# Turning the first expert pair's activations and running its down product before the second pair's rows are turned, with the loads in that order

## The reference

```python
for e in range(N_EXPERTS):
    h = jax.nn.silu(xt @ lp['w_e_gate'][e]) * (xt @ lp['w_e_up'][e])
    y = y + combine[:, e:e + 1] * (h @ lp['w_e_down'][e])
```

## Time and profile before

| what | us |
|---|---|
| median of 3 runs | 783.74 |
| lowest and highest | 783.07, 784.20 |
| span of the profiled execution, first to last instruction | 783.6 |
| TensorE busy | 741.4 (95%) |
| VectorE busy | 408.8 (52%) |
| ScalarE busy | 259.2 (33%) |
| GpSimd busy | 74.4 (9%) |

### The profile page before, as it was taken

One profiled execution on the slowest core, in us unless ns is written; L12 is line 12 of the kernel. 1 busy time (PEld: TensorE's weight loads), 2 busy tenths in 40 slices (PEclk: granted clock), 3 DMA queues, 4 the chain that ended last, 5 costly groups with the idle time before them and its releaser, 6 DMA issues.

```text
span 783.6 us, 12757 instructions
## 1 busy us (share of the span) xinstructions
PE 741.4 (95%) x5288; PEld 576.0 (74%) x5288; DVE 408.8 (52%) x755; ACT 259.2 (33%) x446; POOL 74.4 (9%) x104
## 2 busy tenths in 40 slices
PE   8999999999999999999999999999999997778884
PEld 7999999999999777899999988885333332323322
DVE  6999839986347785665154386554112111114226
ACT  5662351123486645532442341230111111100113
POOL 0100022001011111000000000011121221111100
PEclk9999999999999999999999999999999999999997
DMA  9578326434238433400260694389999999999994
GB/s 342 202 264 316 109 82 106 118 115 151 102 131 323 162 138 118 182 1 2 108 219 12 222 425 189 128 353 345 419 423 424 418 424 424 419 423 425 422 388 161
DMA packets 38143, 190.68 MB, mean 243 GB/s; under 512 B 5914, under 2 KB 7466, under 8 KB 21864
## 3 DMA queue, kind: packets, MB, share of 16 engines
q1 hardware_dynamic: 23696, 148.22, 47.8%
q0 software_dynamic: 11200, 34.98, 13.4%
q10 hardware_dynamic: 3184, 6.60, 2.3%
HBM read 176.17 MB, written 21.41 MB: 252 GB/s over the span
## 4 chain that ended last, share of the span: by engine, by line
PE 76%; DMA 14%; DVE 5%; ACT 3%; issue 1%; SPq 1%; DVEq 0%; ACTq 0%; POOLq 0%
PE ps L662 72%; DMA sb<-in_wexp 11%; PE ps L676 4%; DMA expert_rows<-sb 2%; DVE sb L2763 1%; DMA sb<-expert_rows 1%; DMA sb<-in_xT 1%; DVE sb L2298 1%; DVE sb L2284 1%; SPq L562 1%; ACT sb L1431 1%; ACT sb L1631 1%; DVE sb L2696 0%; ACT sb L1653 0%; ACT sb L1636 0%
## 5 line engine op out<-in xcount | busy, mean ns | idle before, releaser
L662 PE MATMUL ps<-sr 128*128 128x288 f32 (+3 forms) x2906 | 407.3, 300 | 3.5 <-DVE ps L2701 3.0
L662 PEld LDWEIGHTS ps<-sr 128*128 128x128 f32 (+1 forms) x2906 | 388.1, 188 | 18.6 <-issue 5.6
L662 PE MATMUL ps<-sb 128*64 128x512 f32 (+16 forms) x1984 | 296.9, 429 | 28.7 <-DMA sb<-in_wexp 18.1
L662 PEld LDWEIGHTS ps<-sb 128*64 128x64 f32 (+7 forms) x1984 | 148.0, 148 | 149.8 <-issue 124.7
L2632 DVE SCALAR_TENSOR_TENSOR sb<-sb,ps 128x256 f32<-128x256 f32 x16 | 6.7, 421 | 117.7 <-ACT sb L1830 117.7
L676 PEld LDWEIGHTS ps<-sb 128*128 128x128 f32 (+3 forms) x398 | 42.2, 140 | 31.0 <-issue 28.6
L676 PE MATMUL ps<-sb 128*128 128x128 f32 (+3 forms) x398 | 53.7, 273 | 2.3 <-issue 1.4
L2246 DVE TENSOR_TENSOR sr<-sb,sr 128x2048 fp32r<-128x2048 f32 (+1 forms) x17 | 39.3, 2320 | 29.1 <-ACT sr L1545 19.0
L2640 DVE COPY sb<-ps 128x1024 f32<-128x1024 f32 x15 | 18.4, 1225 | 54.5 <-PE ps L662 54.5
L1431 ACT ACTIVATE sb<-ps 128x576 f32<-128x576 f32 (+3 forms) x28 | 21.9, 783 | 67.4 <-PE ps L662 47.4
L2357 DVE SCALAR_TENSOR_TENSOR sb<-sb,ps 128x576 f32<-128x576 f32 x24 | 18.1, 753 | 46.5 <-PE ps L662 46.3
(11 more groups left out here) (291 smaller groups left out, 509.2 us busy)
## 6 DMA issues: line engine op xcount, KB each, us to landing
sb<-in_wexp SPq DMA_DIRECT2D x91, 1024.0 KB, 22.1
sb<-in_wstream SPq DMA_DIRECT2D x33, 1024.0 KB, 5.7
expert_rows<-sb ACTq DMA_DIRECT2D x1, 4608.0 KB, 24.9
sb<-in_mkT POOLq DMA_DIRECT2D x8, 512.0 KB, 7.7
sb<-in_mv POOLq DMA_DIRECT2D x8, 512.0 KB, 5.1
sb<-expert_rows SPq DMA_DIRECT2D x4, 1024.0 KB, 9.0
sb<-in_wexp SPq DMA_DIRECT2D x5, 768.0 KB, 25.4
sb<-in_x SPq DMA_DIRECT2D x4, 512.0 KB, 14.1
```

The lines of the kernel that those rows point to most:

```text
L662: return signed(nc.tensor.matmul(*a, **kw))
```

## The change

For the first pair of each of the two sets, the hidden activations are turned and the down product is made right after `gate_up(i, 1)`, ahead of `turn_rows(i + 1)`. In the second pair nothing of the first is left to do, so the two halves of its gate and up products stand next to each other. From the third pair on the order is the old one. ScalarE's copies and VectorE's results are moved to match, and the load table puts the two down pieces of pair 0 in places 4 and 5, ahead of the four pieces of pair 1, which were 4 to 7 and are now 6 to 9. No operation is added or taken away, and every load has the size that its place had.

```diff
@@ plan_chunks
-            if i > first:
+            if i == first:
+                parts.append([("d", i, 0, x) for x in range(2)])
+            elif i > first + 1:
                 parts.insert(0 if i == end - 1 else 2, [("d", i - 1, 0, x) for x in range(2)])
@@ TensorE
-            def body(i, first, last):
+            def body(i, first, second, last):
...
                 if last:
                     own_rows(2)
-                elif not first:
+                elif not first and not second:
                     turn_hidden(i - 1)
...
+                if first:
+                    turn_hidden(i)
+                    down(i)
                 turn_rows(i + 1)
-                if not first:
+                if not first and not second:
                     down(i - 1)
...
-                    body(i, first=(i == i0), last=(i == i1 - 1))
+                    body(i, first=(i == i0), second=(i == i0 + 1), last=(i == i1 - 1))
@@ ScalarE
-                    if i > i0:
+                    if i > i0 + 1:
                         hidden_turned(i - 1)
                     gate(i)
+                    if i == i0:
+                        hidden_turned(i)
@@ VectorE
                     hidden(i)
-                    if i > i0:
+                    if i == i0:
+                        result(i)
+                    if i > i0 + 1:
                         result(i - 1)
```

## The result

The changed kernel takes 785.0 us (median of 20 runs, 783.36 to 787.67) against 783.63 for the kernel before in the same session (20 runs, 782.0 to 786.04): a ratio of 1.0023, 95% interval 1.0013 to 1.0032, so some 1.8 us slower (the two medians themselves lie 1.4 us apart). The forecast was 783.7, no change. The time lies inside the range, but the change is slower, clear of zero, and I gave 0.12 to a loss of over 0.2%.

What follows compares the result with a forecast made beforehand. The prediction took the full DMA queue from about 545 us to bound the kernel; TensorE's 3.3 us lateness was hidden and the loads lost 0, so 783.7 + 0 = 783.7 us, range 782.4 to 785.9.

Steps and rivals of the forecast that it cites:

- a loss of over 0.2%: Whole kernel: the outcome slower, by more than about 1.6 us; chance 0.12, against 0.84 for same and 0.04 for faster.
- What bounds the kernel: Expert stage: its end is the time from which the DMA queue is full (about 545 us) plus bytes still to move.
- TensorE's steps: First pairs, from 543.40: `down(0)` at 545.85, `gate_up(2, 0)` at 560.87, TensorE 3.3 us late, hidden by 4.1 us of later waits.
- The forecast took the clock to hold: At `down(0)`, after the added waits: 8 matmuls still take 3.58 us; the forecast had chance 0.70.
- The limits: Latest gap-free issue, 2.5 us ahead of the previous landing: load 22 at 546.9, 24 at 552.7, 26 at 557.6, 30 at 568.8.
- 0 us lost: Loads 22 to 30: all go out ahead of their limits, load 22 with 0.3 us left after the gather; nothing lost.
- the clock rival: TensorE's clock falls in 547 to 560, costing 1.7 us once; time 783.7 to 784.5, up to 784.8 with two falls; chance 0.08.
- The gather and the scatter: Around 551 to 553: pair 3's later gather takes 1.24 us off the queue, the earlier first scatter adds 1.24 us.
- The bounds: On time lost in the loads: 0 at least, 1.6 us at most, the whole lateness of load 22 (545.4 - 543.8).
- The signs of being wrong: DMA share under 0.95 in 545 to 560, clock 0.50 in 547 to 560, traces differing before 543 or in last 40 us.
- Span against median: Whole kernel: profiled span 783.6 and median 783.74 differ by 0.14, so the forecast counts from the median.

Runs made afterwards that it cites:

- look_after_2: The changed kernel, unaltered, run once more for its trace; that execution took 784.55 us.
- e_late8: The kernel before, order and loads untouched, with eight dummy products between the first pair's second half and `turn_rows(1)`; ratio to before 1.0086.
- look_before_2: The kernel before, unaltered, run once more for its trace; span 783.3, time 785.1 us.
- a_clock_release: The changed kernel with TensorE's waits in the first pairs filled by 256-column dummy products and loads 22 and 23 released early by a small product; ratio to before 1.0002.
- a_clock: The changed kernel with TensorE's waits in the first pairs filled by dummy products of 256 columns; ratio to before 1.0005.
- c_rows_first: The changed kernel with the second pair's rows turned ahead of the first pair's activations and down product, ScalarE's copies likewise; ratio to before 1.0006.

## Why the prediction was wrong, point by point

- **What bounds the kernel: right up to the last load.** TensorE waits 5.9 us less for weights, so its lateness did not reach the end of the expert stage by itself, and what the queue lost did. But I left out any difference behind the last load, where 0.8 of the 1.8 us between the traces stand; its cause is open.
- **TensorE's steps: right.** Transposes at 544.76 (544.97 forecast, on a stage that began 0.2 earlier), 0.88 us to the down product, 2.21 from turned rows to the product, load 22 at 545.1 (545.4). In look_after_2, where the clock holds, `gate_up(2, 0)` starts 17.5 us after the second half of pair 0, 3.2 later than before, against 3.3 forecast. There the sum held: 416 GB/s.
- **The forecast took the clock to hold: wrong, by a mechanism that I had as a rival.** The clock did fall, 1.7 us were lost on `down(0)`, load 24 went out at 551.3 (551.5 in the rival) and load 26 at 556.8 (557.0). TensorE came 4.9 us late (5.0). I gave it 0.08; it is in 2 of 3 traces. My reason against it was a single wait of 2.75 us elsewhere that left the clock alone. The earlier trace rows already showed the other case, and the clock of the stretch 526 to 530, which I had not put among the rows, showed a fall some 20 us ahead of this place.
- **The limits: the step that failed.** It is the term "0 us lost" of the forecast, and with it the 0 to 0.8 us of the clock rival. I took it that a load leaves no gap if it goes out 2.5 us ahead of the landing of the load before. Load 24 went out 554.9 - 551.3 = 3.6 us ahead of it, load 26 5.0 us ahead of load 25's (561.8), and still 1.3 to 1.7 us of transfer were lost in 30 us. The clock rival was priced at 0 to 0.8 us for that reason; 1.8 came out in all, 1.0 of it up to the last load. The lone load's 5.0 us hold a start in which its engines are counted as busy and move little: share 0.99 at 164 GB/s in 536 to 537 before, 0.91 at 197 in 552 to 553 after. My reading, which no run isolates, is that in a deep queue that start lies beside other loads' transfers, so that the loss is not a step at the limit but grows as the queue thins. e_late8 measures the limits from the other side: 7.1 us of lateness, 6.7 lost where they allow 3.9 to 5.1.
- **The gather and the scatter: no term found.** Putting the scatter back changed nothing that the runs can tell.
- **The bounds.** I bounded the loss by load 22's whole lateness, 1.6 us, and left out load 24's with a fallen clock (8.1 - 5.9 = 2.2 us). That was the larger.
- **The signs of being wrong.** Three of those named came: a share of 0.94 in 550 to 560, a clock of 0.50 at 546 to 549, and a difference in the last 40 us.
- **Span against median.** I took the span of 783.6 for the time of that execution, and nothing for what lies outside the span. The later runs list both: look_before_2 has a span of 783.3 and takes 785.1 us, the changed kernel's 785.2 and 786.97. So the profiled execution of before probably took some 785.4 us, 1.7 above the median; since the forecast was a difference, nothing hung on it.

What stays open: why the clock falls behind these waits in some executions only, beyond the observation that in all five traces with the change's waits it went together with a fall 20 us earlier; why it falls at 526 with TensorE at work; how large a share of the executions has it; and what adds 0.8 us behind the last load. No variant tried here was faster than the kernel before. a_clock_release, a_clock and c_rows_first are the nearest, none of them to be told from it.

## What to carry to other kernels

Don't take the time of a lone load for the point up to which a late release is free: read how long each load takes from issue to landing, and treat one that is near the time of a lone load as already losing. An order that makes the engine that releases buffers wait early in a transfer-bound stage can cost even though that engine catches up later, since the queue doesn't. And where an edit adds waits on TensorE, price the work behind them at both clock levels, and judge from several traces.

## What the runs showed of the hardware that I had not expected

- A dummy product of 512 columns with 128 rows of output took 0.89 us (7.13 / 8, e_late8), the loop's products with 64 rows of output 0.45 (3.58 / 8). The loop's alternate between the two halves of the output rows; whether two of them overlap was not tried.
- The same kernel has its clock fall at 526 to 530 in some executions and not in others: the changed kernel had 0.66 in 525 to 530 in its first and third trace, 1.00 in the second. The fall came with TensorE busy throughout the 10 us ahead of it.
- A DMA share near 1 doesn't mean full speed: 0.99 at 164 GB/s and 0.91 at 197 in one us, 0.94 at 338 GB/s over five.
